# Where weight splits stand in the order of two engines at three changes of stage, in a two-block fp32 kernel

## The chip, the cores and the metric

The kernel runs on one core of one Trainium2 chip. The metric is the time of the program on the device in microseconds (us), as the median of several runs.

## The reference, cut to what matters

256 tokens of width 2048 pass through two blocks, each a mixer followed by a gated feed-forward part (FFN), in fp32. What matters here is what stands between the matrix products:

```
# block one                                   # block two
x1 = x + merged @ w_out                       h  = rms_norm(x2f, attn_norm_w, 1e-5)
h2 = rms_norm(x1, g_ffn)                      p  = h @ w_in_2
x2 = x1 + (silu(gate) * up) @ w_ffn_out       x3 = x2f + y @ w_out_2
x2f = rms_norm(x2, g_final, 1e-6)             h  = rms_norm(x3, ffn_norm_w) ; FFN as in block one
```

`rms_norm(x, g) = x * rsqrt(mean(x*x) + eps) * g`, over the 2048 columns of a token. Between the blocks two norms follow one another: x2 is normed with g_final, and the result, which is also block two's residual, is normed again with attn_norm_w.

## The kernel before, in words

**Products in three terms.** Each fp32 product `x @ w` is made of three matmul passes with a high and a low part of both sides: `xh*wh + xh*wl + xl*wh`. A weight matrix comes in chunks of 512 rows by 512 columns (1 MB, a tile of 128 x 2048). For every chunk SyncE issues a load into one of four ring slots (`raw[j % 4]`), ScalarE copies it to a high part (`hi[j % 2]`, two slots, L1339), VectorE subtracts to get the low part (`lo`, in place of the raw one, L1781), and TensorE runs 48 (`product`, L643 to L646) or 24 (`product_tokens`, L658 to L660) matmuls on it. A high part can be made only once the chunk two before is used up, a load can start once the chunk four before is.

**Order.** Every engine has its own program, written out by hand: nothing reorders it. An engine waits on semaphores in the order of that program, so a step that waits holds up all that stands behind it on the same engine. `Gemm` numbers chunks through the whole kernel; `chunks(g, i, j0, j1)` on ScalarE makes high parts, the function of the same name on VectorE low parts.

**A norm** before a product is split up by quarters (512 columns, 128 x 1024 elements). For each quarter: the residual is updated by VectorE from PSUM (L2057, L2125), ScalarE sums its squares (`squares`, L1323, two instructions and two reads of the sum), TensorE turns it (`turn_x`, L604, 8 transposes), VectorE multiplies by the gain column (`gained`, L1744, 4 instructions), ScalarE makes the high part of the activation (`high`, L1329), VectorE the low part (`low_part`, L1750). The root of the mean is applied behind the product: `inverse_root` makes it, `root_rows` writes it on a diagonal (L1771), TensorE spreads it over rows (`rstd_rows`, L630, behind the fourth chunk), and VectorE copies those rows out (L1774) for the strips to be scaled with.

**Changes of stage that matter here:**

- *Start.* `in1` (block one's input product) begins with four chunks, one for each quarter of the norm. Behind the fourth, TensorE turns parameters and spreads the root (L620, L630). VectorE's program then reads: root, `root_rows(0)` with its wait for TensorE, a copy of the parameters (L1847), and only then the low part of chunk 4.
- *Output product into FFN* (`wo1` into `up1`, `wo2` into `up2`), through `out_ffn`. The output product has four strips of four chunks. When a strip's end is two chunks back, ScalarE runs `residual_high`: `squares`, then `high`, which waits for `gained`, which waits for the turn, which TensorE does after the first chunk of the next strip. The high part of the weights that comes next stands behind that. The pattern occurs four times in each block.
- *FFN's down product into block two's input product* (`dn1` into `in2`). The last four chunks of `dn1` end one quarter each (`down_out`). A quarter of the residual gets x2 (`X`), then `XG = X * g_final` (L2127), which is what TensorE turns; the gain column is attn_norm_w. ScalarE sums the squares of both, `X` and `XG`. SyncE loads four chunks of `in2`, then waits for all sixteen sums of squares (`n_sq` at 16; the tiles share memory), loads two pieces of `w_lora` (L482, L483), and only behind them chunk 4 of `in2` and the rest. From the end of `dn1` on, GpSimd builds masks (L578, L540, L580).

`to_slot`, `f` and `taken` take strips out of PSUM. Waits such as `wait_ge(chunks_used, n)` mean that TensorE has finished chunk n.

Of the kernel before, what the change touches and what calls it, by code (L numbers as in the profile page):

```python
# [12 lines left out]
ALU = mybir.AluOpType  # L13
# [6 lines left out]
KT = D // P  # L20
# [48 lines left out]
def build(nc, a, out):  # L69
    ctx = ExitStack()  # L70
    with ctx:
# [527 lines left out]
        def _(pe):  # L599
# [160 lines left out]
            def downs(g, n, n_norm):  # L760
# [17 lines left out]

# [16 lines left out]
            def last_of_down():  # L795
                pe.wait_ge(xg_ready, 4)
                turn_x(3, 3, XG)

# [515 lines left out]
        def _(act):  # L1314
# [25 lines left out]

            def split(g, i, out_of, j0=0):

                for j in range(j0, g.per):
                    chunks(g, i, j, j + 1)
                    if j == 1 and not (isinstance(i, int) and i == 0):
                        out_of(i - 1, g.ns - 1)
                    elif j > 1 and j - 2 in g.ends:
                        out_of(i, g.ends[j - 2])

# [129 lines left out]

            def residual_high(g, n):  # L1480
                def f(i, s):
                    squares(2 * i + s, squared[1], strips_out, g.strip(i, s) + 1)
                    high(n, 2 * i + s, U[1])
                return f

            def ffn_sigmoid(g, n, i):
# [39 lines left out]
            out_ffn(wo1, up1, dn1, 1, 0, 2)  # L1526
            chunks(dn1, dn1.bodies - 1, 0, 4)

            for q in range(4):
                squares(q, squared[0], x_ready, 1 + q)  # L1530
                squares(q, squared2, xg_ready, 1 + q, XG, ssq2)
# [200 lines left out]
        def _(dve):  # L1732
# [34 lines left out]

            def root_rows(n):
# [3 lines left out]
                last.then_inc(n_diag, 1)  # L1772
                dve.wait_ge(n_sum, n + 1)
                V.tensor_copy(rstd[:], bank(7)[:, 0:T]).then_inc(rows_read, 1)  # L1774
# [96 lines left out]

            chunks(in1, 0, 4, 5)
            to_slot(0, 0)
# [246 lines left out]

            def down_out(g, q, count):

                dve.wait_ge(chunks_used, g.end - 3 + q)
                c = slice(q * CN, (q + 1) * CN)
                V.tensor_tensor(X[:, :, c], X[:, :, c], token_pair(q), ALU.add).then_inc(x_ready, 1)  # L2125
                dve.wait_ge(x_ready, count)
# [4 lines left out]
            chunks(dn1, dn1.bodies - 1, 0, 3)  # L2131
            dve.wait_ge(gain_landed, 16)
            down_out(dn1, 0, 1)
            chunks(dn1, dn1.bodies - 1, 3, 4)
            down_out(dn1, 1, 2)
            gained(2, 0, 0, U[0], "attn_norm_w_2")
            low_part(2, 0, U[0])
            down_out(dn1, 2, 3)
            gained(2, 1, 1, U[0], "attn_norm_w_2")
            low_part(2, 1, U[0])  # L2140
            chunks(in2, 0, 0, 1)
            down_out(dn1, 3, 4)
            gained(2, 2, 2, U[0], "attn_norm_w_2")
            low_part(2, 2, U[0])
            chunks(in2, 0, 1, 2)
            gained(2, 3, 3, U[0], "attn_norm_w_2")
            low_part(2, 3, U[0])
            chunks(in2, 0, 2, 4)
# [38 lines left out]

            chunks(in2, 0, 4, 5)
            f(0, 0)
            for t in range(2):  # L2190
# [408 lines left out]
```

## Time and profile before

| | us |
|---|---|
| median of 3 runs | 3015.83 (3013.49 to 3017.86) |
| the profiled execution: its own time | 3021.99 |
| its span in the trace | 3020.2 |
| TensorE busy (share of the span) | 2930.2 (97%), 18850 matmuls |
| VectorE busy | 1605.0 (53%) |
| ScalarE busy | 1165.7 (39%) |
| GpSimd busy | 49.5 (2%) |
| DMA, mean over the span | 166 GB/s |

The span is that of one execution; engine shares are averages over stages of different kinds. A matmul's duration in the trace reaches beyond the start of the next one, since they overlap: steps are best taken from start to start. The granted clock of TensorE is 1.00 where it runs at 2.4 GHz and 0.50 at 1.2 GHz.

### The profile page before, as it was taken

The numbers are of one execution on the slowest core, as the hardware profiler recorded it, in microseconds if no ns is written. First come the engines' busy times: TensorE is split into PE (matmuls) and PEld (weight loads), VectorE is DVE, ScalarE is ACT, GpSimd is POOL, SyncE is SP. The second block draws the span as 40 slices with busy tenths as digits, with TensorE's granted clock in tenths as the row PEclk, the third lists the DMA queues.
The fourth block names the chain that finished last, engine by engine and source line by source line (L and its number), as shares of the span: only waits on it lengthen the run. The fifth ranks groups of instructions, "written<-read, shape, count | busy, mean of one in ns | idle before, by whom it ended". The sixth has DMA issues, their size and how long they took to land.

```text
span 3020.2 us, 42955 instructions
## 1 busy us (share of the span) xinstructions
PE 2930.2 (97%) x18850; PEld 2521.2 (83%) x18850; DVE 1605.0 (53%) x1331; ACT 1165.7 (39%) x956; POOL 49.5 (2%) x119
## 2 busy tenths in 40 slices
PE   7999999999999999999999999899799999999998
PEld 7999788888778888888879999898677888888887
DVE  4657545445554545444455767754455454544445
ACT  3345443343443333433344433323234333343333
POOL 0000000000000000010001000000000000000000
PEclk9999999999999999999999999898799999999999
DMA  6556556666555555555554544100145555555554
GB/s 198 167 161 183 151 162 195 186 191 194 181 178 184 194 182 193 188 187 195 195 195 159 166 143 154 43 4 31 56 153 178 184 193 183 193 188 187 195 195 167
DMA packets 257288, 501.00 MB, mean 166 GB/s; under 512 B 12176, under 2 KB 17627, under 8 KB 256763
## 3 DMA queue, kind: packets, MB, share of 16 engines
q1 hardware_dynamic: 257147, 498.87, 51.4%
q8 instruction: 120, 1.97, 0.3%
q14 instruction: 21, 0.17, 0.0%
HBM read 496.74 MB, written 2.10 MB: 165 GB/s over the span
## 4 chain that ended last, share of the span: by engine, by line
PE 93%; DVE 5%; ACT 1%; issue 1%; DMA 0%; SPq 0%; ACTq 0%; DVEq 0%
PE psum L658 22%; PE psum L660 22%; PE psum L659 22%; PE psum L643 5%; PE psum L645 5%; PE psum L646 5%; PE psum L1070 3%; DVE weight_lo L1781 2%; ACT weight_hi L1339 1%; PE psum L956 1%; PE psum L709 1%; PE psum L950 0%; DVE u_ffn L1744 0%; PE psum L604 0%; DVE u_in L1744 0%
## 5 line engine op out<-in xcount | busy, mean ns | idle before, releaser
L1781 DVE TENSOR_TENSOR weight_lo<-weight_raw,weight_hi 128x2048 fp32r<-128x2048 f32 x460 | 1054.1, 2292 | 1141.4 <-ACT weight_hi L1339 1140.6
L1339 ACT ACTIVATE weight_hi<-weight_raw 128x2048 fp32r<-128x2048 f32 x460 | 881.0, 1916 | 1486.1 <-PE psum L660 1184.9
L658 PE MATMUL psum<-weight_hi,h_both 128*128 128x512 f32 x1856 | 725.3, 391 | 3.2 <-DVE weight_lo L1781 3.2
L660 PE MATMUL psum<-weight_hi,h_both 128*128 128x512 f32 x1856 | 722.5, 389 | 0.0
L659 PE MATMUL psum<-weight_lo,h_both 128*128 128x512 f32 x1856 | 722.1, 389 | 0.0
L643 PE MATMUL psum<-h_both,weight_hi 128*128 128x256 f32 x1408 | 406.9, 289 | 18.9 <-DVE weight_lo L1781 18.7
L658 PEld LDWEIGHTS psum<-weight_hi,h_both 128*128 128x128 f32 x1856 | 348.5, 188 | 75.1 <-issue 4.0
L660 PEld LDWEIGHTS psum<-weight_hi,h_both 128*128 128x128 f32 x1856 | 348.4, 188 | 72.7
L659 PEld LDWEIGHTS psum<-weight_lo,h_both 128*128 128x128 f32 x1856 | 348.6, 188 | 71.4
L645 PE MATMUL psum<-h_both,weight_lo 128*128 128x256 f32 x1408 | 403.2, 286 | 0.0
L646 PE MATMUL psum<-h_both,weight_hi 128*128 128x256 f32 x1408 | 403.0, 286 | 0.0
L643 PEld LDWEIGHTS psum<-h_both,weight_hi 128*128 128x128 f32 x1408 | 275.3, 196 | 25.0 <-issue 16.5
L645 PEld LDWEIGHTS psum<-h_both,weight_lo 128*128 128x128 f32 x1408 | 275.6, 196 | 0.1
L646 PEld LDWEIGHTS psum<-h_both,weight_hi 128*128 128x128 f32 x1408 | 275.1, 195 | 0.0
L658 PE MATMUL psum<-weight_hi,ffn_hi 128*128 128x512 f32 x672 | 261.9, 390 | 0.0
L660 PE MATMUL psum<-weight_hi,ffn_lo 128*128 128x512 f32 x672 | 261.4, 389 | 0.0
L659 PE MATMUL psum<-weight_lo,ffn_hi 128*128 128x512 f32 x672 | 261.4, 389 | 0.0
L660 PEld LDWEIGHTS psum<-weight_hi,ffn_lo 128*128 128x128 f32 x672 | 126.1, 188 | 26.4
L658 PEld LDWEIGHTS psum<-weight_hi,ffn_hi 128*128 128x128 f32 x672 | 126.1, 188 | 26.3 <-issue 0.6
L659 PEld LDWEIGHTS psum<-weight_lo,ffn_hi 128*128 128x128 f32 x672 | 126.1, 188 | 26.0
L660 PE MATMUL psum<-weight_hi,y_lo 128*128 128x512 f32 x320 | 126.3, 395 | 0.0
L658 PE MATMUL psum<-weight_hi,mixed_hi 128*128 128x512 f32 x256 | 103.4, 404 | 19.3 <-DVE weight_lo L1781 19.3
(512 smaller groups left out, 2305.6 us busy)
## 6 DMA issues: line engine op xcount, KB each, us to landing
weight_raw<-in_w_in SPq DMA_DIRECT2D x144, 1024.0 KB, 5.5
weight_raw<-in_w_ffn_in SPq DMA_DIRECT2D x88, 1024.0 KB, 5.0
weight_raw<-in_w_ffn_out SPq DMA_DIRECT2D x44, 1024.0 KB, 5.1
weight_raw<-in_ffn_w_gate SPq DMA_DIRECT2D x44, 1024.0 KB, 5.1
weight_raw<-in_ffn_w_up SPq DMA_DIRECT2D x44, 1024.0 KB, 5.1
weight_raw<-in_ffn_w_down SPq DMA_DIRECT2D x44, 1024.0 KB, 5.1
weight_raw<-in_w_out SPq DMA_DIRECT2D x32, 1024.0 KB, 5.1
weight_raw<-in_w_branch_rnn SPq DMA_DIRECT2D x8, 1024.0 KB, 5.1
```

What stands on the lines that cost most here:

```text
L643: mm(acc[:, f, :], wh[:, k, c], xh, start=(start and k == 0 and f % 2 == 0), stop=False, skip_group_check=True)
L645: mm(acc[:, f, :], wl[:, k, c], xh, start=False, stop=False, skip_group_check=True)
L646: last = mm(acc[:, f, :], wh[:, k, c], xl, start=False, stop=(stop and k == CK - 1), skip_group_check=True)
L658: mm(acc[:, t, :], xh[:, c], wh[:, k, :], start=(start and k == 0), stop=False, skip_group_check=True)
L659: mm(acc[:, t, :], xh[:, c], wl[:, k, :], start=False, stop=False, skip_group_check=True)
L660: last = mm(acc[:, t, :], xl[:, c], wh[:, k, :], start=False, stop=(stop and k == CK - 1), skip_group_check=True)
L709: last = tr(pair(2)[:, k, t * P:(t + 1) * P], act_up[:, t, k * P:(k + 1) * P], ident[:])
L956: last = mm(bank(b0 + (n - n0) // 2)[:, (n % 2) * T:(n % 2 + 1) * T], sel[:, n * P:(n + 1) * P], rows[:], start=(n % 2 == 0), stop=True, s ...
L1070: last = mm(o[r, u * 64:(u + 1) * 64], lhs(r, u0 + u), rhs(r, u0 + u), start=(u == 0), stop=True, skip_group_check=True)
L1339: A(hi[j % g.hi][:], raw[j % g.ring][:], ACT.Copy).then_inc(hi_ready, 1)
L1781: V.tensor_tensor(lo[r][:], raw[r][:], hi[j % g.hi][:].bitcast(F32), ALU.subtract).then_inc(lo_ready, 1)
```

## The change

Nothing is computed that was not before, but for one product of two columns of parameters; the number of matmuls, loads and table loads stays as it was. Cut to the core:

```diff
@@ TensorE: downs(), last_of_down() @@
-                            pe.wait_ge(xg_ready, j)
-                            turn_x(j - 1, j - 1, XG)
+                            pe.wait_ge(x_ready, j)
+                            turn_x(j - 1, j - 1, X)
...
@@ ScalarE: split() knows a later step, one chunk behind the first @@
+                    for d, f in ((2, out_of), (3, later)):
...
+                        if not first and j + g.per - d in g.ends:
+                            f(i - 1, g.ends[j + g.per - d])
+                        elif j >= d and j - d in g.ends:
+                            f(i, g.ends[j - d])
...
-                f = residual_high(wo, n_norm)
-                split(wo, 0, f, rhs)
-                split(wo, 1, f)
-                chunks(up, 0, 0, 2)
-                f(1, 1)
-                chunks(up, 0, 2, 4)
+                squared_of = lambda i, s: squares(2 * i + s, squared[1], strips_out, wo.strip(i, s) + 1)
+                high_of = lambda i, s: high(n_norm, 2 * i + s, U[1])
+                split(wo, 0, squared_of, rhs, high_of)
+                split(wo, 1, squared_of, 0, high_of)
+                chunks(up, 0, 0, 1)
+                chunks(up, 0, 1, 2)
+                squared_of(1, 1)
+                chunks(up, 0, 2, 3)
+                high_of(1, 1)
+                chunks(up, 0, 3, 4)
...
@@ ScalarE, dn1 into in2 @@
-            chunks(dn1, dn1.bodies - 1, 0, 4)
-            for q in range(4):
-                squares(q, squared[0], x_ready, 1 + q)
-                squares(q, squared2, xg_ready, 1 + q, XG, ssq2)
-                high(2, q, U[0])
-                if 0 < q < 3:
-                    chunks(in2, 0, q - 1, q)
-            chunks(in2, 0, 2, 4)
+            chunks(dn1, dn1.bodies - 1, 0, 3)
+            squares_x(0)
+            chunks(dn1, dn1.bodies - 1, 3, 4)
+            high(2, 0, U[0])
+            squares_x(1)
+            chunks(in2, 0, 0, 1)
+            squares_gained(0)
+            high(2, 1, U[0])
+            squares_x(2)
+            chunks(in2, 0, 1, 2)
+            high(2, 2, U[0])
+            squares_x(3)
+            chunks(in2, 0, 2, 3)
+            high(2, 3, U[0])
+            squares_gained(1)
+            chunks(in2, 0, 3, 4)
+            squares_gained(2)
+            squares_gained(3)
...
@@ VectorE: root_rows() is cut in two, the diagonals (root_diagonals) and the wait with the copy (root_rows) @@
             inverse_root(1, 4, EPS1)
+            root_diagonals()
+            chunks(in1, 0, 4, 5)
             root_rows(0)
...
-            chunks(in1, 0, 4, 5)
             to_slot(0, 0)
...
@@ VectorE, dn1 into in2: down_out() only updates X, times_gain() makes XG @@
+            settle(V.tensor_tensor(par1[:, c1:c1 + KT], par1[:, c1:c1 + KT], par1[:, c2:c2 + KT], ALU.mult))
...
+            chunks(dn1, dn1.bodies - 1, 0, 2)
+            down_out(0)
+            chunks(dn1, dn1.bodies - 1, 2, 3)
+            down_out(1)
+            next_gained(0)
+            chunks(dn1, dn1.bodies - 1, 3, 4)
...
+            times_gain(0)
+            down_out(2)
+            next_low(0)
+            next_gained(1)
+            chunks(in2, 0, 0, 1)
+            next_low(1)
+            down_out(3)
+            next_gained(2)
+            chunks(in2, 0, 1, 2)
+            next_low(2)
+            times_gain(1)
+            next_gained(3)
+            chunks(in2, 0, 2, 3)
+            next_low(3)
+            times_gain(2)
+            times_gain(3)
+            chunks(in2, 0, 3, 4)
...
-                root_rows(1)
+            root_diagonals()
...
             chunks(in2, 0, 4, 5)
+            root_rows(1)
             f(0, 0)
```

Here c1 and c2 are the columns of attn_norm_w and g_final: the gain that `next_gained` applies to the turned X is their product. What moves, in three places:

**ScalarE, output product into FFN, first strip.** raw2 is the slot of chunk 6, raw1 that of chunk 5, `squares_ffn` the squares of the first quarter, `h_both<-u_ffn` the high part of the activation. Before:

```order
L1339 ACTIVATE weight_hi1_58<-weight_raw1_50 128x2048
L1323 ACTIVATE squares_ffn_66,sum_squares_99<-residual_61 128x512 x2
L1329 ACTIVATE h_both_62<-u_ffn_64 128x1024
L1339 ACTIVATE weight_hi0_57<-weight_raw2_51 128x2048
L1339 ACTIVATE weight_hi1_58<-weight_raw3_52 128x2048
```

Changed:

```order
L1339 ACTIVATE weight_hi1_58<-weight_raw1_50 128x2048
L1323 ACTIVATE squares_ffn_66,sum_squares_99<-residual_61 128x512 x2
L1339 ACTIVATE weight_hi0_57<-weight_raw2_51 128x2048
L1329 ACTIVATE h_both_62<-u_ffn_64 128x1024
L1339 ACTIVATE weight_hi1_58<-weight_raw3_52 128x2048
```

The high part of chunk 6 has changed places with that of the activation; VectorE's order is the same in both there.

**VectorE, dn1 into in2.** raw2 and raw3 are the last two chunks of dn1, raw0 is the first of in2. Before:

```order
L1781 TENSOR_TENSOR weight_lo2_55<-weight_raw2_51,weight_hi0_57 128x2048
L2125 TENSOR_TENSOR residual_61<-residual_61,psum 128x2x512
L2127 TENSOR_TENSOR x_gained_68<-residual_61,gain_row_69 128x2x512
L1781 TENSOR_TENSOR weight_lo3_56<-weight_raw3_52,weight_hi1_58 128x2048
L2125 TENSOR_TENSOR residual_61<-residual_61,psum 128x2x512
L2127 TENSOR_TENSOR x_gained_68<-residual_61,gain_row_69 128x2x512
L1744 TENSOR_SCALAR u_in_63<-psum,par1_97 128x256 x4
L1750 TENSOR_TENSOR h_both_62<-u_in_63,h_both_62 128x1024
L2125 TENSOR_TENSOR residual_61<-residual_61,psum 128x2x512
L2127 TENSOR_TENSOR x_gained_68<-residual_61,gain_row_69 128x2x512
L1744 TENSOR_SCALAR u_in_63<-psum,par1_97 128x256 x4
L1750 TENSOR_TENSOR h_both_62<-u_in_63,h_both_62 128x1024
```

Changed:

```order
L2146 TENSOR_TENSOR residual_61<-residual_61,psum 128x2x512
L1801 TENSOR_TENSOR weight_lo2_55<-weight_raw2_51,weight_hi0_57 128x2048
L2146 TENSOR_TENSOR residual_61<-residual_61,psum 128x2x512
L1761 TENSOR_SCALAR u_in_63<-psum,par1_97 128x256 x4
L1801 TENSOR_TENSOR weight_lo3_56<-weight_raw3_52,weight_hi1_58 128x2048
L2152 TENSOR_TENSOR x_gained_68<-residual_61,gain_row_69 128x2x512
L2146 TENSOR_TENSOR residual_61<-residual_61,psum 128x2x512
L1767 TENSOR_TENSOR h_both_62<-u_in_63,h_both_62 128x1024
L1761 TENSOR_SCALAR u_in_63<-psum,par1_97 128x256 x4
L1801 TENSOR_TENSOR weight_lo0_53<-weight_raw0_49,weight_hi0_57 128x2048
L1767 TENSOR_TENSOR h_both_62<-u_in_63,h_both_62 128x1024
```

`x_gained` no longer stands in front of each turn, and the low part of in2's first chunk (raw0) has come ahead of the second `h_both`; before, it stands behind the last row shown.

**ScalarE, end of the same place.** Before, the last rows ahead of the root:

```order
L1329 ACTIVATE h_both_62<-u_in_63 128x1024
L1339 ACTIVATE weight_hi1_58<-weight_raw1_50 128x2048
L1323 ACTIVATE squares_in_65,sum_squares_99<-residual_61 128x512 x2
L1323 ACTIVATE squares_gained_67,sum_squares_gained_100<-x_gained_68 128x512 x2
L1329 ACTIVATE h_both_62<-u_in_63 128x1024
L1339 ACTIVATE weight_hi0_57<-weight_raw2_51 128x2048
L1339 ACTIVATE weight_hi1_58<-weight_raw3_52 128x2048
```

Changed:

```order
L1339 ACTIVATE weight_hi0_57<-weight_raw2_51 128x2048
L1329 ACTIVATE h_both_62<-u_in_63 128x1024
L1323 ACTIVATE squares_gained_67,sum_squares_gained_100<-x_gained_68 128x512 x2
L1339 ACTIVATE weight_hi1_58<-weight_raw3_52 128x2048
L1323 ACTIVATE squares_gained_67,sum_squares_gained_100<-x_gained_68 128x512 x4
```

The last sums of squares, which SyncE's wait counts, stand behind the high parts of all four first chunks of in2, where they stood behind those of the first two.

## Rows read from the trace of the kernel before

**Rows 1.** The page's waits of TensorE: engine, line, releaser: us in total, times, longest.

```profile
PE psum L658 <- DVE weight_lo L1781: 22.5, 10, 6.6
PE psum L643 <- DVE weight_lo L1781: 18.7, 10, 4.8
```

**Rows 2.** Timeline of TensorE, second strip of wo1: start, duration, instruction [idle before, releaser].

```profile
776.82 1.03 PE L604 MATMUL psum<-ident,residual 128*128 128x128 f32 x8
777.61 0.48 PE L658 MATMUL psum<-weight_hi,mixed_hi 128*128 128x512 f32 x1
...
784.83 0.50 PE L658 MATMUL psum<-weight_hi,mixed_hi 128*128 128x512 f32 x1 [1.52 <-DVE weight_lo L1781]
...
801.29 1.04 PE L604 MATMUL psum<-ident,residual 128*128 128x128 f32 x8
```

**Rows 3.** Timeline of ScalarE at the same place.

```profile
779.59 1.06 ACT L1329 ACTIVATE h_both<-u_ffn 128x1024 fp32r<-128x1024 f32 x1 [4.81 <-DVE u_ffn L1744]
780.55 1.90 ACT L1339 ACTIVATE weight_hi<-weight_raw 128x2048 fp32r<-128x2048 f32 x1
```

**Rows 4.** Timeline of VectorE at the same place.

```profile
777.89 1.66 DVE L1744 TENSOR_SCALAR u_ffn<-psum,par 128x256 f32<-128x256 f32 x4 [2.02 <-PE psum L604]
782.49 2.29 DVE L1781 TENSOR_TENSOR weight_lo<-weight_raw,weight_hi 128x2048 fp32r<-128x2048 f32 x1 [2.93 <-ACT weight_hi L1339]
```

**Rows 5.** Timeline of TensorE behind the fourth chunk of in1.

```profile
43.90 0.65 PE L630 MATMUL psum<-rstd_diag,ones 128*128 128x128 f32 x4
47.91 0.58 PE L643 MATMUL psum<-h_both,weight_hi 128*128 128x256 f32 x1 [3.36 <-DVE weight_lo L1781]
```

**Rows 6.** Timeline of VectorE and ScalarE at the same place.

```profile
44.58 0.42 DVE L1774 COPY rstd<-psum 128x256 f32<-128x256 f32 x1 [5.71 <-PE psum L630]
45.56 2.29 DVE L1781 TENSOR_TENSOR weight_lo<-weight_raw,weight_hi 128x2048 fp32r<-128x2048 f32 x1
...
38.06 1.90 ACT L1339 ACTIVATE weight_hi<-weight_raw 128x2048 fp32r<-128x2048 f32 x1
```

**Rows 7.** TensorE by stretches: start:end, length, busy (matmuls), granted clock, DMA share, GB/s.

```profile
47.91:62.26 14.35, 14.35 (x96) 0.79 0.82 246
1585.00:1593.00 8.00, 8.00 (x49) 0.69 0.00 1
1594.18:1600.01 5.83, 5.83 (x48) 1.00 0.85 285
1616.84:1624.84 8.00, 8.00 (x54) 0.79 0.14 52
2095.50:2109.00 13.50, 13.50 (x165) 0.51 0.00 1
...
2192.60:2200.60 8.00, 8.00 (x25) 0.69 0.01 2
```

**Rows 8.** Timeline of TensorE, dn1 into in2.

```profile
1566.37 1.09 PE L604 MATMUL psum<-ident,x_gained 128*128 128x128 f32 x8 [1.34 <-DVE x_gained L2127]
...
1585.00 0.55 PE L643 MATMUL psum<-h_both,weight_hi 128*128 128x256 f32 x1 [4.85 <-DVE weight_lo L1781]
...
1616.84 0.36 PE L643 MATMUL psum<-h_both,weight_hi 128*128 128x256 f32 x1 [2.94 <-DVE weight_lo L1781]
```

**Rows 9.** Waits of SyncE's queue, 1560 to 1660 us.

```profile
SPq L482 <- ACT squares_gained L1323: 14.5, 1, 14.5
```

**Rows 10.** Timeline of ScalarE, the last sum of squares and chunk 4 of in2.

```profile
1593.45 0.61 ACT L1323 ACTIVATE squares_gained<-x_gained 128x512 f32<-128x512 f32 x1
...
1607.89 1.91 ACT L1339 ACTIVATE weight_hi<-weight_raw 128x2048 fp32r<-128x2048 f32 x1 [1.64 <-DMA weight_raw<-in_w_in]
```

**Rows 11.** Timeline of VectorE and of GpSimd while the masks are built.

```profile
1586.02 1.23 DVE L2127 TENSOR_TENSOR x_gained<-residual,gain_row 128x1024 f32<-128x1024 f32 x1
1591.74 2.29 DVE L1781 TENSOR_TENSOR weight_lo<-weight_raw,weight_hi 128x2048 fp32r<-128x2048 f32 x1 [0.58 <-ACT weight_hi L1339]
...
1580.11 16.48 POOL L540 TENSOR_SCALAR_AFFINE_SELECT chunk_masks_upper<-chunk_masks_upper 128x64 f32<-128x64 f32 x28
```

More of the change, by code:

```diff
@@ L795, in last_of_down @@
             def last_of_down():
-                pe.wait_ge(xg_ready, 4)
-                turn_x(3, 3, XG)
+                pe.wait_ge(x_ready, 4)
+                turn_x(3, 3, X)
             def forget_logits():
@@ L1339, in chunks, with split @@
                     A(hi[j % g.hi][:], raw[j % g.ring][:], ACT.Copy).then_inc(hi_ready, 1)
-            def split(g, i, out_of, j0=0):
+            def split(g, i, out_of, j0=0, later=None):
                 for j in range(j0, g.per):
                     chunks(g, i, j, j + 1)
[L1345 to L1348, printed above, removed]
+                    first = isinstance(i, int) and i == 0
+                    for d, f in ((2, out_of), (3, later)):
+                        if f is None:
+                            continue
+                        if not first and j + g.per - d in g.ends:
+                            f(i - 1, g.ends[j + g.per - d])
+                        elif j >= d and j - d in g.ends:
+                            f(i, g.ends[j - d])
             def strip_done(e, g, i, s):
@@ L1478, in _ @@
             merged_high(3)
[L1480 to L1484, printed above, removed]
             def ffn_sigmoid(g, n, i):
@@ L1526, in _, with squares_x, squares_gained @@
             out_ffn(wo1, up1, dn1, 1, 0, 2)
-            chunks(dn1, dn1.bodies - 1, 0, 4)
-            for q in range(4):
+            def squares_x(q):
                 squares(q, squared[0], x_ready, 1 + q)
+            def squares_gained(q):
                 squares(q, squared2, xg_ready, 1 + q, XG, ssq2)
-                high(2, q, U[0])
-                if 0 < q < 3:
-                    chunks(in2, 0, q - 1, q)
-            chunks(in2, 0, 2, 4)
+            chunks(dn1, dn1.bodies - 1, 0, 3)
[16 more added lines that the diff above has]
+            squares_gained(3)
             root(3, rcol1)
@@ L1766, in inverse_root, with root_diagonals @@
                 dve.wait_ge(ready, made)
-            def root_rows(n):
+            def root_diagonals():
                 for t in range(2):
@@ L1772, in root_rows @@
                 last.then_inc(n_diag, 1)
+            def root_rows(n):
                 dve.wait_ge(n_sum, n + 1)
@@ L2119, in out_ffn, with down_out, times_gain @@
                     chunks(dn, i, 0, 4)
-            def down_out(g, q, count):
-                dve.wait_ge(chunks_used, g.end - 3 + q)
+            def down_out(q):
+                dve.wait_ge(chunks_used, dn1.end - 3 + q)
                 c = slice(q * CN, (q + 1) * CN)
                 V.tensor_tensor(X[:, :, c], X[:, :, c], token_pair(q), ALU.add).then_inc(x_ready, 1)
-                dve.wait_ge(x_ready, count)
+            def times_gain(q):
+                c = slice(q * CN, (q + 1) * CN)
+                dve.wait_ge(x_ready, q + 1)
                 V.tensor_tensor(XG[:, :, c], X[:, :, c], gain_row[:, c].unsqueeze(1).to_broadcast([P, 2, CN]),
@@ L2130, in _ @@
             out_ffn(wo1, up1, dn1, 1, "g_ffn", EPS1, 0, 3)
-            chunks(dn1, dn1.bodies - 1, 0, 3)
-            dve.wait_ge(gain_landed, 16)
[L2133 to L2140, printed above, removed]
+            c1, c2 = col["attn_norm_w_2"], col["g_final"]
+            settle(V.tensor_tensor(par1[:, c1:c1 + KT], par1[:, c1:c1 + KT], par1[:, c2:c2 + KT], ALU.mult))
+            next_gained = lambda q: gained(2, q, q, U[0], "attn_norm_w_2")
+            next_low = lambda q: low_part(2, q, U[0])
+            chunks(dn1, dn1.bodies - 1, 0, 2)
[4 more added lines that the diff above has]
+            chunks(dn1, dn1.bodies - 1, 3, 4)
+            dve.wait_ge(gain_landed, 16)
+            times_gain(0)
+            down_out(2)
+            next_low(0)
+            next_gained(1)
             chunks(in2, 0, 0, 1)
-            down_out(dn1, 3, 4)
-            gained(2, 2, 2, U[0], "attn_norm_w_2")
-            low_part(2, 2, U[0])
+            next_low(1)
+            down_out(3)
+            next_gained(2)
             chunks(in2, 0, 1, 2)
-            gained(2, 3, 3, U[0], "attn_norm_w_2")
-            low_part(2, 3, U[0])
-            chunks(in2, 0, 2, 4)
+            next_low(2)
[6 more added lines that the diff above has]
+            chunks(in2, 0, 3, 4)
             inverse_root(3, 16, EPS1, rcol1)
```

## The prediction, made before the changed kernel ran

> **What bounds the kernel now.** I read the page first: TensorE is busy 97% of the span, so time can only come from its pauses, from what they do to its clock, or from its work, which stays as it is. The waits of TensorE then say who ends the pauses: twenty waits on `weight_lo`, 41.2 us together [rows 1]. The timelines say where they are. Four of 1.5 to 1.6 us stand in each passage from the output product to the FFN (one of them: [rows 2]), one of 3.36 us behind the start's fourth chunk [rows 5], and pauses of 1.34, 4.85 and 2.94 us in the passage from dn1 to in2 [rows 8]. These are the places that the change touches. The rest of the 41.2 us (6.62 us before wo2 above all) it leaves alone.
>
> The windows show the second price of a pause [rows 7]. At granted clock 1.00, which is 2.4 GHz, 48 matmuls take 5.83 us, 0.1215 us each. Behind the 4.85 us pause 49 of them take 8.00 us instead of 5.95, since the clock stands at 1.2 GHz for some of it: 2.05 lost. By the same sum 2.7 us are lost behind the 3.36 us pause (96 in 14.35 instead of 11.66) and 1.4 behind that of 2.94 (54 in 8.00 instead of 6.56). Behind the 6.62 us before wo2 it is 2.3 (25 of the 512-wide, at 0.228 each [rows 2]: 5.7 instead of 8.00).
>
> **Part A, output product into FFN, eight places.** In one of them the turn begins at 776.82, the next chunk at 777.61, the chunk after that at 784.83, and the next turn at 801.29 [rows 2]. The last three chunks so take 16.46, 5.49 each; the first would take about as much, 5.54 with the slower first matmuls behind a turn, and end at 783.15. The place costs 784.83 - 783.15 = 1.68, and some 0.1 for the restart. Cause: ScalarE holds `high` for 4.81 us until `gained` is done at 779.55, and only then makes the high part of chunk 6, at 780.55 [rows 3, 4]; VectorE has the low part from 782.49 to 784.78 [rows 4]. In the changed order nothing holds that high part back but its slot, free when the turn begins at about 776.9: done 778.8. VectorE still has `gained` in front (to 779.55), so the low part is done at 779.55 + 2.25 = 781.8, 1.35 us ahead of need. `high` follows at 779.6 to 780.65, `low_part` behind the weight's low part to 783, the next chunk's high part at 783.3, when its slot comes free, as before. Nothing new is late. Bounds for a place: 1.5 (the pause alone) and 1.8; I take 1.75, since the starts bear it out. **Eight places: 14.0 us** (12.2 to 14.4).
>
> **Part B, start.** The high part of chunk 4 is done at 39.96, the rows are copied only at 44.58 behind 5.71 us of waiting, and the low part begins at 45.56 [rows 6]. Now it stands ahead of the wait: 40.0 to 42.3. TensorE goes on when its last transposes let it, 0.15 us before their recorded end at 44.55, so at 44.4 instead of 47.91 [rows 5]: 3.5 us. The clock's 2.7 go too. VectorE's copies and the first strip's evacuation then end near 46.8, the low part of chunk 5 near 49.4, and TensorE needs it at 44.4 + 5.8 = 50.2. **6.2 us** (3.5 if the clock falls all the same).
>
> **Part C, dn1 into in2.** Here the early steps gain much and the end gives most of it back. TensorE no longer waits for `x_gained`: the turn follows at 1564.9 instead of 1566.37, its last turn in dn1 comes at 1577.6, and in2 could start at 1578.4, if chunk 0's low part is there. VectorE, in the new order with durations start to start of 1.2 (residual and gain) [rows 11], 1.6 (`gained`) and 2.2 (low part of weights) [rows 4], and 1.15 (low part of the activation, a tile of the size of x_gained): from 1571.4, when the second turn has freed the third quarter, its steps follow with no gap. The third residual, low 0, gained 1 and chunk 0's low part end at 1577.6. So in2 starts at 1578.4 instead of 1585.00, 6.6 us earlier and at 2.4 GHz. Its four chunks end at 1584.2, 1590.9, 1596.7 and 1602.5 (5.83 each, [rows 7], one turn between the first two); the low parts of chunks 1, 2 and 3 are done at 1583.8, 1590.0 and 1595.8, each ahead of need, by 0.9 to 1.2 us.
>
> But then chunk 4 is missing. SyncE's queue waited 14.5 us for the last sum of squares [rows 9], and the loads of w_lora and of chunk 4 stand behind that wait. The last sum ends at 1594.06, ScalarE finds chunk 4 at 1607.89 [rows 10], 13.83 us later, with TensorE's speed having no part in it. In the new order the last sum comes *later*: from 1571.4 VectorE has 5 x 1.2 + 4 x 1.15 + 3 x 1.6 + 3 x 2.2 = 22.0 us to do up to the last x_gained, 1593.4; ScalarE makes chunk 3's high part to 1592.9 (its slot is freed at 1590.9) and the last two pairs of squares to 1595.3. Then 13.8 for the loads, 1.9 for the high part [rows 10], 2.3 for the low part [rows 4] and 0.2 of handshakes: TensorE starts chunk 4 at 1613.6 instead of 1616.84. It has stood since 1603.1, 10.5 us, longer than any pause shown, and the clock will fall. Earlier start 3.2; the loss at 1616.84, 1.4, goes; one of about 2.3, as behind the 6.62 us pause, comes. **2.3 us.** Bounds: if each of the four activation low parts waits 1.1 us for ScalarE, as it does between `gained` and `low_part` before, the last sum comes 4.4 later and the part gives -2.1; if the clock stays up, +4.6. The product of the two gain columns (0.2 us) and the later rows of the root lie beside the wait for chunk 4 and cost nothing; should that cover go, they have the 10.5 us pause to fill first.
>
> Masks are built during this. x_gained (1.23) and a weight's low part (2.29) run at their usual speed while GpSimd works from 1580.11 to 1596.6 [rows 11], so I take VectorE's durations as they are. The Trainium skill speaks against that: the GPSIMD Engine Reference, Specifications, says that GpSimd shares its SBUF interfaces with VectorE and contends with VectorE's instructions that have two SBUF inputs. By that rule x_gained and both kinds of low part would slow down under the masks; it is a rival below.
>
> **Sum.** 14.0 + 6.2 + 2.3 = 22.5 us. The profiled execution took 3021.99 (span 3020.2 and 1.8 around it), so it would take 2999.5; it lies 6.2 above the median of 3015.83, so **the median goes to 2993.3**.
>
> **Rivals.**
> 1. *The last sum is later than I make it* (ScalarE and VectorE wait for one another in the dense new order, up to the bound above). Part C gives about -1: 2996.6. For it: `low_part` waited for `high` at every quarter before. Against: weight parts now fill those waits. 0.10.
> 2. *VectorE still comes late in part A*, since `gained` stays in front of chunk 6's low part and the margin is 1.35 us. Half of A remains: 3000.3. Against: all eight places have the same rows within 0.05 us. 0.08.
> 3. *Chunk 4 does not bind*: then the 10.5 us pause and the 2.3 lost behind it go too, and C is worth 15.1: 2980.5. Against: the queue's wait and the 13.83 us behind it [rows 9, 10], whose order the change leaves. 0.03.
> 4. *GpSimd slows VectorE.* From 1579 to 1594 three gain steps of 1.2, two low parts of weights of 2.2 and three of activations of 1.15 would double, 11.4 us, and the last sum is that much later: C gives 3.2 - 11.4 + 1.4 - 2.3 = -9.1, so 3004.7. Against: the speeds under the masks [rows 11]. 0.02.
> 5. *Slower:* the clock stays down after the pause before chunk 4. To end over 6 us slower it must lose 28.5 us more than I reckon, which at 1.2 GHz takes 57 us of running; with 60, 3023. For it: the pause is longer than any I have rows for. Against: the longest low stretch found is 13.5 us [rows 7], and behind 6.62 us the clock was back within 8. 0.04. The skill's page TensorE: Matmul & The Clock Gate, Seeing it yourself, warns that the gate has been seen stuck at a low setting for over 50 us; with 50, an estimate by that page, C would lose 25 and the time come to about 3016, no change.
> 6. *No effect within 6 us*: the pauses move to other chunks. 0.03.
>
> **How the numbers follow.** My forecast gets 0.70. About 0.2% (6 us) is what a measurement of this kernel can tell from no change. Faster by more: the forecast and rivals 1 to 4, 0.70 + 0.10 + 0.08 + 0.03 + 0.02 = 0.93; same 0.03; slower 0.04. The range goes from 2986 (the forecast with A and C at their upper ends, 2.7, less 2 for the chain of part C and 2 for the medians' own spread) to 3003 (rivals 1 and 2, plus 2 to 3 of spread); rivals 3 to 6 lie outside, 0.12.
>
> **What would show it.** Right: no wait of 1.5 us on `weight_lo` between turns of `residual` in either passage, and turns there 22.7 apart instead of 24.5; no pause at 44 us; in2's first chunk starting near 1565 (1578.4 less block one's half of A, 7.0, and B, 6.2) at clock 1.00, chunks 0 to 3 in one run; then one pause of about 10 us, ended by a low part whose high part waited for a load; SyncE still waiting for `squares_gained`. Wrong: a pause before chunk 4 shorter than 6 us or longer than 14, waits on `weight_lo` left in part A, or low clock for more than 10 us behind the pause.

## The result, and the profile after

Over four runs of each in turn, the changed kernel took 2993.29 us (median; 2987.71 to 2997.93) and the kernel before 3016.69 (3013.49 to 3017.86). The ratio is 0.9924, 95% interval 0.9906 to 0.9942: faster by 23.4 us, where 22.5 was forecast. The profiled execution took 2997.93 with a span of 2996.2, which is 24.0 less than the span before.

The page's first part, its waits of TensorE (rows of part 5) and SyncE's queue between 1545 and 1645 us (engine, line, releaser: us in total, times, longest), answer to [rows 1, 9]:

```profile
PE 2923.0 (98%) x18850; PEld 2518.7 (84%) x18850; DVE 1604.5 (54%) x1332; ACT 1166.9 (39%) x956; POOL 53.0 (2%) x119
...
L643 PE MATMUL psum<-h_both,weight_hi 128*128 128x256 f32 x1408 | 404.8, 288 | 16.3 <-DVE weight_lo L1801 16.3
...
L658 PE MATMUL psum<-weight_hi,mixed_hi 128*128 128x512 f32 x256 | 102.4, 400 | 10.2 <-DVE weight_lo L1801 10.2
```

```profile
SPq L482 <- ACT squares_gained L1323: 17.3, 1, 17.3
```

The work of every engine is the same. TensorE's waits on low parts of weights fell from 41.2 us to 26.5. Of these 9.9 are one new pause and 6.6 the one before wo2, which the change leaves alone. SyncE now waits longer for the sums of squares than before (17.3 for 14.5).

**Output product into FFN.** TensorE around the same turn as in [rows 2]; the four chunks between the second row and the next turn have no pause among them:

```profile
770.75 1.03 PE L604 MATMUL psum<-ident,residual 128*128 128x128 f32 x8
771.54 0.48 PE L658 MATMUL psum<-weight_hi,mixed_hi 128*128 128x512 f32 x1
...
793.41 0.82 PE L604 MATMUL psum<-ident,residual 128*128 128x128 f32 x6
```

ScalarE and VectorE there, the rows that answer to [rows 3, 4]:

```profile
771.01 1.92 ACT L1339 ACTIVATE weight_hi<-weight_raw 128x2048 fp32r<-128x2048 f32 x1 [2.31 <-PE psum L660]
773.52 1.07 ACT L1329 ACTIVATE h_both<-u_ffn 128x1024 fp32r<-128x1024 f32 x1 [0.59 <-DVE u_ffn L1761]
```

```profile
771.83 1.66 DVE L1761 TENSOR_SCALAR u_ffn<-psum,par 128x256 f32<-128x256 f32 x4 [2.02 <-PE psum L604]
773.40 2.28 DVE L1801 TENSOR_TENSOR weight_lo<-weight_raw,weight_hi 128x2048 fp32r<-128x2048 f32 x1
```

The high part of the weights begins 0.26 us after the turn, when its slot comes free, not 3.7 after it. The low part ends at 775.68. The chunk that wants it follows the one begun at 771.54, which takes 5.54, so from 777.08: 1.4 us to spare. From turn to turn it is 22.66 instead of 24.47.

**Start.** VectorE makes the low part at 40.18 and only then waits for the rows, and TensorE's next chunk stands directly behind its transposes:

```profile
40.18 2.29 DVE L1801 TENSOR_TENSOR weight_lo<-weight_raw,weight_hi 128x2048 fp32r<-128x2048 f32 x1 [1.12 <-ACT weight_hi L1339]
44.76 0.42 DVE L1794 COPY rstd<-psum 128x256 f32<-128x256 f32 x1 [2.29 <-PE psum L630]
```

```profile
44.08 0.65 PE L630 MATMUL psum<-rstd_diag,ones 128*128 128x128 f32 x4
44.48 0.36 PE L643 MATMUL psum<-h_both,weight_hi 128*128 128x256 f32 x1
```

**dn1 into in2.** TensorE, where [rows 8] had three pauses:

```profile
1564.25 1.04 PE L604 MATMUL psum<-ident,residual 128*128 128x128 f32 x8
1565.05 0.36 PE L643 MATMUL psum<-h_both,weight_hi 128*128 128x256 f32 x1
...
1599.54 0.55 PE L643 MATMUL psum<-h_both,weight_hi 128*128 128x256 f32 x1 [9.91 <-DVE weight_lo L1801]
```

The first chunk of in2 starts 19.95 us earlier than before (1585.00); 13.3 of them were won ahead of this place, by A and B. Four chunks run without a break. Then one pause of 9.91 us comes, and behind it the clock is low for a while. The windows (columns as in [rows 7], with the busy time of every engine after the length: TensorE, its weight loads, VectorE, ScalarE, GpSimd) show equal lengths after the start's fourth chunk, at full clock, and behind this pause:

```profile
44.48:56.16 11.68, 11.68 (x99) 11.55 (x97) 8.46 (x16) 4.90 (x4) 0.00 (x0) 1.00 0.98 289
1599.54:1611.22 11.68, 11.68 (x80) 11.68 (x81) 7.61 (x6) 5.03 (x5) 0.00 (x0) 0.80 0.50 167
```

80 matmuls at 0.1215 us are 9.7, so 2.0 of the 11.68 were lost. ScalarE says why the pause is there, as in [rows 10]: the last sum of squares, the read of it, and chunk 4 of in2, which it finds 13.1 us behind the end of the squares at 1582.03 (13.83 before):

```profile
1581.42 0.61 ACT L1323 ACTIVATE squares_gained<-x_gained 128x512 f32<-128x512 f32 x1
...
1595.16 1.91 ACT L1339 ACTIVATE weight_hi<-weight_raw 128x2048 fp32r<-128x2048 f32 x1 [10.23 <-DMA weight_raw<-in_w_in]
```

SyncE's own rows show what lies between the two:

```profile
1582.15 0.37 SPq L482 DMA_DIRECT2D w_lora<-in_w_in  x1
1582.56 2.03 SPq L483 DMA_DIRECT2D w_lora<-in_w_in  x1
1584.64 40.60 SPq L460 DMA_DIRECT2D weight_raw<-in_w_in  x8
```

The first of the eight loads in the last row is chunk 4's. It lands 10.5 us after its issue, where the median of such loads is 5.5. Just ahead of it stand 2.4 MB of w_lora, which land 8.8 and 9.2 us after theirs; that they are what makes it late is read from these times, not tested. Before, the same load took 11.4.

**Where the 24.0 us of the two spans went**, by starts on TensorE:

| stretch | before | after | less |
|---|---|---|---|
| start to the forget logits (L802) | 62.26 | 56.16 | 6.10 |
| L802 to wo1's first turn | 714.56 | 714.59 | -0.03 |
| wo1's first to fourth turn | 73.41 | 68.00 | 5.41 |
| fourth turn to the first w_lora product (L914) | 802.72 | 797.45 | 5.27 |
| L914 to wo2's first chunk | 539.65 | 539.39 | 0.26 |
| from there to wo2's first turn | 18.74 | 18.96 | -0.22 |
| wo2's first to fourth turn | 73.49 | 67.99 | 5.50 |
| fourth turn to the end | 735.37 | 733.66 | 1.71 |

Each place of part A is worth 1.80 (5.41 / 3), and the fourth place of each block lies in the row below its three. So A has 5.41 + 1.80 + 5.50 + 1.71 = 14.4, B 6.1, and C 5.27 - 1.80 = 3.5.

### The profile page after: what moved, and what is told of

It reads as the page before. It is cut to its first block, busy times and chain, and to the rows that moved or that the text cites. A ratio compares the mean times of both kernels' runs of the same rounds, so it can differ in the third digit from the quotient of the medians.

```text
span 2996.2 us, 42957 instructions
## 1 busy us (share of the span) xinstructions
PE 2923.0 (98%) x18850; PEld 2518.7 (84%) x18850; DVE 1604.5 (54%) x1332; ACT 1166.9 (39%) x956; POOL 53.0 (2%) x119
## 4 chain that ended last, share of the span: by engine, by line
PE 95%; DVE 3%; ACT 1%; DMA 0%; issue 0%; SPq 0%; DVEq 0%; ACTq 0%
PE psum L658 23%; PE psum L660 23%; PE psum L659 23%; PE psum L643 5%; PE psum L645 5%; PE psum L646 5%; PE psum L1070 3%; PE psum L956 1%; DVE weight_lo L1801 1%; PE psum L709 1%; PE psum L950 0%; PE psum L604 0%; DMA weight_raw<-in_w_in 0%; ACT weight_hi L1339 0%; PE psum L1034 0%; PE psum L872 0%
## 5 line engine op out<-in xcount | busy, mean ns | idle before, releaser
L658 PEld LDWEIGHTS psum<-weight_hi,ffn_hi 128*128 128x128 f32 x672 | 126.1, 188 | 26.5 <-issue 0.6
```

The source lines that it names most:

```text
L658: mm(acc[:, t, :], xh[:, c], wh[:, k, :], start=(start and k == 0), stop=False, skip_group_check=True)
```

## Experiments

Every kernel here computes all of the reference. "C's stretch" is the time from wo1's fourth turn to L914, with 1.8 us added for kernels that have part A, so that it compares with the 802.7 of before. The kernel before was run beside every batch: 3019.69 for the first four labels, 3015.90 for the next four, 3018.05 for the last two.

**The parts one by one.** Each is the kernel before with one part of the change put in, and `changed_again` is the changed kernel. `...` in a diff stands for lines that are not shown.

`only_strips` (part A):

```diff
...
-                split(wo, 1, f)
-                chunks(up, 0, 0, 2)
-                f(1, 1)
-                chunks(up, 0, 2, 4)
+                split(wo, 1, squared_of, 0, high_of)
+                chunks(up, 0, 0, 1)
+                chunks(up, 0, 1, 2)
+                squared_of(1, 1)
+                chunks(up, 0, 2, 3)
+                high_of(1, 1)
+                chunks(up, 0, 3, 4)
```

`only_start` (part B):

```diff
             inverse_root(1, 4, EPS1)
+            root_diagonals()
+            chunks(in1, 0, 4, 5)
             root_rows(0)
...
-            chunks(in1, 0, 4, 5)
             to_slot(0, 0)
```

`only_between` (part C) has the turns of X, both new orders from dn1 to in2, and the later rows:

```diff
-                            turn_x(j - 1, j - 1, XG)
+                            turn_x(j - 1, j - 1, X)
...
-            root_rows(1)
+            root_diagonals()
...
             chunks(in2, 0, 4, 5)
+            root_rows(1)
```

> The kernel before with part A alone (ScalarE makes the high part of chunk 6 ahead of that of the activation). My theory: the eight pauses of 1.5 us on weight_lo go, turn to turn falls from 24.5 to 22.7 us, the time falls by 14.0 to 14.4 us; the start and the passage from dn1 to in2 keep their pauses (3.36, 4.85, 2.94 us). Rival (VectorE comes late all the same): half of it, 7 us. Rival (the strips only pay together with the rest): under 3 us.

> The kernel before with part B alone (low part of chunk 4 of in1 ahead of the wait for the spread root). My theory: the pause of 3.36 us at 44 us goes and with it the low clock behind it, so 6.1 us: 3.4 for the pause and 2.7 for the clock. Rival (the clock falls there all the same, from what ran before): 3.4 us only.

> The changed kernel with parts A and B undone: part C alone. My theory: in2's first chunk starts 6.6 us earlier against the turns of dn1 and chunk 4 only 3.2 to 4.0 us earlier, behind a pause of about 10 us ended by the load; net 3.0 to 3.7 us, within the noise of the medians. Rival (the gain of 6.6 us and the clock carry through): 10 us or more.

> The changed kernel once more, on the chip of the other three. If the parts are independent, its gain over the kernel before is the sum of the three: 14.2 + 6.1 + 3.7 = 24 us by the trace, 0.8%. The four runs seen spread over 10 us (2987.7 to 2997.9), those before over 4.4. If that spread is the pause's, it shows in the length of the pause before chunk 4 or in the clock behind it.

| | median (runs) | range | ratio to before [95%] | span of the profile |
|---|---|---|---|---|
| only_strips | 3002.74 (6) | 2993.46 to 3012.46 | 0.9941 [0.9917, 0.9965] | 3010.5 |
| only_start | 3010.60 (10) | 3001.16 to 3016.02 | 0.9975 [0.9964, 0.9987] | 2999.4 |
| only_between | 3013.84 (10) | 3004.40 to 3022.99 | 0.9984 [0.9971, 0.9998] | 3005.2 |
| changed_again | 2993.55 (4) | 2988.19 to 2997.45 | 0.9920 [0.9903, 0.9936] | 2986.5 |

The three ratios multiplied give 0.9900, with some 0.003 of uncertainty, against 0.9920: the parts add up within what the runs can tell, and each is a gain by itself, `only_between` just clear of none. The traces are sharper than the medians. `only_strips` has its turns 22.67 us apart and no other pause gone (it reaches L802 at 61.45, for 62.26 before; C's stretch is 803.9). `only_start` reaches L802 at 55.77. In `only_between` C's stretch is 800.1, 2.6 less than before where 3.0 to 3.7 was expected, with this row in place of the pause of 2.94:

```profile
1612.38 0.55 PE L643 MATMUL psum<-h_both,weight_hi 128*128 128x256 f32 x1 [10.20 <-DVE weight_lo L1799]
```

How far C's stretch can be trusted shows in four kernels in which nothing in it should change, and which all keep the pause of 2.94 us: 802.7 before and in `only_start`, 803.9 in `only_strips`, 801.3 in `loads_ahead_before` below. Behind that pause the same 288 matmuls up to L914 take 36.11, 36.08, 37.27 and 34.63 us, at granted clocks of 0.95, 0.95, 0.92 and 1.00. So differences of the stretch under some 1.3 us say nothing.

The single spans are a warning: `only_start` has a profile 20.8 us shorter than before's, though its own place gives 6.5. The last section says where that comes from.

**Is the 9.91 us pause the load of chunk 4?** By my account SyncE's wait for the sums holds it back. So let two more chunks be loaded ahead of that wait, in the changed kernel (`loads_ahead`) and in the kernel before (`loads_ahead_before`):

```diff
-            load(in2, 0, 0, 4)
+            load(in2, 0, 0, 6)
             sp.wait_ge(n_sq, 16)
...
-            load(in2, 0, 4)
+            load(in2, 0, 6)
```

> The changed kernel, with SyncE issuing the loads of chunks 4 and 5 of in2 ahead of its wait for the sixteen sums of squares (before, behind the wait and behind w_lora). My theory: that wait is what holds chunk 4 back, so the 9.9 us pause goes and the low clock behind it (2.1 us): 12 us faster than the changed kernel, about 2981 by medians; w_lora lands at its old time and is not needed earlier, chunk 6 lands just in time. Rival (something else holds chunk 4, VectorE's rows of the root or ScalarE's order): a pause of over 5 us stays. Rival (w_lora or chunk 6 come late instead): the pause moves to chunk 6, and 3 to 8 us are gained.

> The same edit of SyncE's order on the kernel before. My theory: there the pause of 2.94 us before chunk 4 is ended by VectorE, whose low part stands behind its wait for the spread root (high part ready since 1609.8, low part begun at 1614.4), so the earlier load changes nothing: 0 +- 1 us. Rival (the load binds there too): 3 to 4 us faster.

`loads_ahead` took 2983.19 (2975.98 to 2985.85, four runs), ratio 0.9888 [0.9870, 0.9906]: the lowest median of all kernels here, about 10 us below the changed one. SyncE's wait fell to 4.1 us, since the queue reaches it later, and TensorE goes from the fourth chunk's transposes straight into chunk 4; one pause of 0.60 us stands before chunk 5.

```profile
SPq L482 <- ACT squares_gained L1323: 4.1, 1, 4.1
```

```profile
1588.43 0.61 PE L630 MATMUL psum<-rstd_diag,ones 128*128 128x128 f32 x4
1588.81 0.36 PE L643 MATMUL psum<-h_both,weight_hi 128*128 128x256 f32 x1
1595.40 0.39 PE L643 MATMUL psum<-h_both,weight_hi 128*128 128x256 f32 x1 [0.60 <-DVE weight_lo L1801]
```

C's stretch is 788.0, 11.3 below the changed kernel's. So the pause is the load's. The edit takes chunk 4 past two things at once, though, SyncE's wait and w_lora. No kernel here leaves it behind the wait and ahead of w_lora. By an estimate from the rows above it would then be issued at 1582.15 and land 5.5 us later, 7.5 us sooner than it did, and most of the pause would go; w_lora is first used at 1603.47. The same edit in the kernel before did nothing: 3018.86 (3013.41 to 3022.17, ten runs), ratio 1.0005 [0.9994, 1.0016], C's stretch 801.3, which is the clock's doing as said above. ScalarE now made chunk 4's high part when TensorE freed its slot (this row of its timeline), 5.50 us ahead of the transposes at 1609.94. In [rows 10], where it waited for the load, it was 5.40 ahead of them, so the load had been 0.1 late. TensorE's pause stayed to the hundredth:

```profile
1604.44 1.92 ACT L1339 ACTIVATE weight_hi<-weight_raw 128x2048 fp32r<-128x2048 f32 x1 [1.56 <-PE psum L646]
```

```profile
1613.48 0.36 PE L643 MATMUL psum<-h_both,weight_hi 128*128 128x256 f32 x1 [2.94 <-DVE weight_lo L1781]
```

So the 2.94 us in the kernel before were not the load's. VectorE in `loads_ahead_before` shows whose they were: its copy of the rows waits 6.79 us for TensorE's transposes, and the low part of chunk 4 stands behind it.

```profile
1610.59 0.42 DVE L1774 COPY rstd<-psum 128x256 f32<-128x256 f32 x1 [6.79 <-PE psum L630]
1611.05 2.29 DVE L1781 TENSOR_TENSOR weight_lo<-weight_raw,weight_hi 128x2048 fp32r<-128x2048 f32 x1
```

**Are the rows of the root the cause?** `only_rows_later` moves nothing else in the kernel before; `rows_early_again` puts them back in the changed one.

```diff
             settle(V.tensor_tensor(rcol[:], rcol[:], rcol1[:], ALU.mult))
-            root_rows(1)
+            root_diagonals()
...
             chunks(in2, 0, 4, 5)
+            root_rows(1)
             f(0, 0)
```

> The kernel before, with root_rows(1) moved behind the low part of chunk 4 of in2 and nothing else. My theory: the 2.94 us pause shrinks to 0 to 0.3 us (high part 1609.8, low part to 1612.1, TensorE there at 1613.2) and the 1.4 us lost to the clock go: 4.3 us faster, as much as all of part C nets. Rival: the load or ScalarE hold chunk 4 to about the same time, under 1 us.

> The changed kernel, with root_rows(1) back ahead of the low part of chunk 4 of in2. My theory: TensorE spreads the root at 1589.0 and the high part of chunk 4 is ready only at 1597.1, so the copy is long done: same as the changed kernel within 0.3 us in the trace. Rival: the order of the two costs something here too, 1 to 4 us slower.

In `only_rows_later` the pause is gone:

```profile
1613.20 0.61 PE L630 MATMUL psum<-rstd_diag,ones 128*128 128x128 f32 x4
1613.57 0.36 PE L643 MATMUL psum<-h_both,weight_hi 128*128 128x256 f32 x1
```

C's stretch is 799.0, 3.7 less than before: this one line gives as much as the whole of part C (3.5; 2.6 in `only_between`), as far as the stretch can tell. The median is 3016.61 (3010.65 to 3018.00, ten runs), ratio 0.9992 [0.9982, 1.0002], too little to tell by runs alone. In `rows_early_again` the stretch is 798.6 with a pause of 9.99, and the median 2991.21 (2982.04 to 2997.97, four runs), ratio 0.9916 [0.9884, 0.9947]: in the changed kernel, where the load is last, the place of the rows is worth nothing.

**Both small edits without part C.** If they did it all, part C's new order would be idle. `loads_and_rows_before` is the kernel before with both:

```diff
-            load(in2, 0, 0, 4)
+            load(in2, 0, 0, 6)
...
             chunks(in2, 0, 4, 5)
+            root_rows(1)
```

> The kernel before with both small edits: loads of chunks 4 and 5 of in2 ahead of SyncE's wait, and root_rows(1) behind the low part of chunk 4. It closes the square of four: reorder of part C or not, loads ahead or not. My theory: without the reorder TensorE does not get to chunk 4 before 1613.2, so the loads ahead add nothing to the 3.7 us that the rows give: last turn of wo1's stage to the first product with w_lora 799.0 us, as without them. With the reorder they took it from 797.5 to 786.2. Rival (loads ahead are worth 11 us by themselves): 788.

The stretch is 799.0 again, the median 3015.34 (3008.21 to 3018.01, ten runs), ratio 0.9986 [0.9976, 0.9996]. With rows and loads out of the way the new order is worth 799.0 - 788.0 = 11.0 us, and all of it comes from its early steps. Counted from wo1's fourth turn, in2's first chunk starts 6.7 us earlier (728.1 us behind it with the 1.8 added, for 734.8), where [rows 8] had pauses of 1.34 and 4.85, and from there to the root's transposes TensorE needs 23.97 instead of 28.29 us. Without the loads ahead all of that is given back in one pause.

**Or bring the last sum forward.** In the changed kernel `sums_early` makes all of x_gained and its squares before the last quarter of the activation, and leaves the loads where they are.

```diff
             chunks(in2, 0, 2, 3)
-            high(2, 3, U[0])
             squares_gained(1)
-            chunks(in2, 0, 3, 4)
             squares_gained(2)
             squares_gained(3)
+            high(2, 3, U[0])
+            chunks(in2, 0, 3, 4)
...
             times_gain(1)
+            times_gain(2)
+            times_gain(3)
             next_gained(3)
```

> The changed kernel with SyncE's order as it is, but the last three x_gained and their sums of squares ahead of the last activation quarter on VectorE and ScalarE. My theory (the wait for the sixteen sums holds chunk 4 back): the last sum comes about 5.3 us earlier (1576.7 for 1582.0 in the changed kernel's trace), a pause of about 1.4 us appears before chunk 2 of in2, and chunk 4 starts 5 us earlier all the same, with a pause of 3 to 5 us before it instead of 10. Rival (chunk 4 comes when its load has time in the queues, whatever the sums): chunk 4 starts at the same time or, with the new pause, 1.4 us later.

Median 2989.99 (2983.84 to 2993.59, four runs), ratio 0.9891 [0.9875, 0.9908]. TensorE's timeline has two pauses:

```profile
1578.64 0.36 PE L643 MATMUL psum<-h_both,weight_hi 128*128 128x256 f32 x1 [1.24 <-DVE weight_lo L1801]
...
1595.24 0.55 PE L643 MATMUL psum<-h_both,weight_hi 128*128 128x256 f32 x1 [4.40 <-DVE weight_lo L1801]
```

SyncE's wait fell from 17.3 to 11.9, the last sum was 5.4 us earlier, chunk 2 came 1.24 late as expected, and chunk 4 started 4.1 earlier than in `changed_again`, both counted from wo1's fourth turn. Of the 5.4 us 1.3 were lost on the way, since chunk 4 was found 14.5 us behind the last squares, not 13.2: its load landed 11.9 us after its issue, not 10.5. C's stretch is 795.2, 4.2 less than 799.4 in `changed_again` and 7.2 more than in `loads_ahead`, which the ratios (0.9891 and 0.9888) do not tell apart. The chain of last sum, queue and load is shown from both of its ends: the pause shrinks with an earlier sum, and goes with an earlier load.

## Why the prediction held, and where it did not

**The total, 22.5 forecast, 23.4 by medians and 24.0 by spans.** That the medians came within 1 us is partly luck: the interval of the ratio reaches from 17.5 to 28.4 us. The parts, read from stretches of the trace, are what the forecast can be held against.

**Part A, 14.0 forecast, 14.4 measured (14.5 in `only_strips`' turns).** The mechanism held at all eight places. The low part's margin was 1.4 us where 1.35 was reckoned. The term was 1.75 a place and each gave 1.80, the upper bound: 0.28 went beside the pause of 1.52, where the 1.75 leaves 0.23.

**Part B, 6.2 forecast, 6.1 measured.** TensorE went on at 44.48 (44.4 forecast), and the low clock is gone. But the second half of that term was partly luck. Six kernels with the old start show how long TensorE needs from its restart to L802: 14.35, 14.33, 13.10, 13.07, 12.99 and 11.70 us, against 11.68 without a pause. Behind the same pause of 3.36 us the clock costs from nothing to 2.7, 1.6 on average. I took one execution's 2.7 for the price. By that average B is worth about 3.6 + 1.6 = 5.2, with 3.6 for the restart, which comes 6.50 us behind the start of the fourth chunk (37.98) instead of 10.12 (37.79).

**Part C, 2.3 forecast, 3.5 measured.** Step by step, with the forecast's times moved by its own 13.2 us of A and B:

| | forecast | measured |
|---|---|---|
| first chunk of in2 | 1565.2 | 1565.05 |
| last squares end | 1582.1 | 1582.03 |
| from there to chunk 4 found | 13.8 | 13.1 |
| chunk 4 starts | 1600.4 | 1599.54 |
| pause before it | 10.5 | 9.91 |
| clock lost behind it | 2.3 | 2.0 |

The step that was mis-sized is the passage of the load, 13.8 for 13.1, and the clock took 0.3 less; that is nearly all of the 1.2. The passage is no constant: the landing of chunk 4's load, behind w_lora, is 10.5 us of it here, and it was 11.4 before and 11.9 in `sums_early`. Nor is 3.5 sharper than the 1.3 us by which C's stretch varies: `changed_again` gives 3.3, `only_between` 2.6.

One step failed in substance, though it cost the sum nothing. I wrote of the later rows of the root that they "lie beside the wait for chunk 4 and cost nothing", and for the kernel before I named only the load as what chunk 4 waits for, which makes the pause of 2.94 us the load's. It belonged to those rows. Before, chunk 4's high part was done at 1609.8 [rows 10], so its low part could have ended at 1612.1, and TensorE came for it only behind the root's transposes of 1613.29. Before, too, VectorE stood waiting for those transposes, with the low part behind the wait:

```profile
1613.29 0.61 PE L630 MATMUL psum<-rstd_diag,ones 128*128 128x128 f32 x4
```

```profile
1613.94 0.42 DVE L1774 COPY rstd<-psum 128x256 f32<-128x256 f32 x1 [6.79 <-PE psum L630]
1614.40 2.29 DVE L1781 TENSOR_TENSOR weight_lo<-weight_raw,weight_hi 128x2048 fp32r<-128x2048 f32 x1
```

The end of the pause was right for the changed kernel alone, because there the load is later than either. So the forecast held the total, and would have been wrong about any smaller version of the change: the rows alone give 3.7, the loads alone nothing.

**Rivals.** *The last sum later* did not come: the squares ended within 0.1 us of the forecast, and the four activation low parts never waited for ScalarE. *VectorE late in A*: no pause at any place. *Chunk 4 does not bind*: it does, but the price set for it was right. I gave C 15.1 us without that pause, and `loads_ahead` has 802.7 - 788.0 = 14.7. *The clock stays down*: 2.0 us were lost. *No effect*: no. *GpSimd slows VectorE*: not here. The masks now run from 1565.25, under nearly all of VectorE's chain, and its steps take what they took:

```profile
1565.25 19.85 POOL L540 TENSOR_SCALAR_AFFINE_SELECT chunk_masks_upper<-chunk_masks_upper 128x64 f32<-128x64 f32 x28
```

```profile
1571.38 1.25 DVE L2152 TENSOR_TENSOR x_gained<-residual,gain_row 128x1024 f32<-128x1024 f32 x1
...
1574.12 2.32 DVE L1801 TENSOR_TENSOR weight_lo<-weight_raw,weight_hi 128x2048 fp32r<-128x2048 f32 x1
...
1585.36 1.68 DVE L1788 TENSOR_SCALAR rstd_diag<-ident,rstd_col 128x128 f32<-128x128 f32 x2
```

1.25 and 2.32 us stand against 1.23 and 2.29 [rows 11]. The Trainium skill's GPSIMD Engine Reference, Specifications, has the two engines contend over their SBUF interfaces for just such instructions; for these masks the trace shows 1 to 2% of it on VectorE's side.

## What to carry to other kernels

When work is moved earlier in front of a wait that stays, the gain is paid back at that wait: look up what is queued behind it, and whether it needs the wait at all, and move that too (here two loads on SyncE's queue, 10 us in the medians, for a change of two numbers). A pause names only its last link, so before a pause is put down to one cause, look at what the engine that ends it was itself waiting for, and check that the suspected input was in fact late. And small edits of a few us are better judged by one stretch of the trace, from one landmark to the next, than by medians of a kernel whose executions differ by 10 us in another place, once kernels that leave the stretch alone have shown how much it varies by itself.

## What the runs showed of the hardware that I had not expected

**The same work takes two lengths.** From L914 to wo2's first chunk all twelve profiles run the same instructions. Seven took 537.6 to 544.1 us, five 525.0 to 529.4, with no relation to the part of the change that they have. The windows show a difference of granted clock, in `only_strips` and in `changed_again`:

```profile
1646.07:2190.18 544.11, 503.81 (x6864) 467.09 (x6863) 337.42 (x444) 181.34 (x215) 7.71 (x8) 0.91 0.26 83
```

```profile
1636.61:2165.87 529.26, 488.94 (x6865) 456.81 (x6863) 337.42 (x444) 181.41 (x215) 7.73 (x8) 0.94 0.27 85
```

And it falls where TensorE has no pause, in the middle of a row of narrow products (`g_up`, each second one with 32 rows). In `only_strips`:

```profile
1729.43 0.70 PE L943 MATMUL psum<-lora,g_up 128*128 128x256 f32 x2
1730.06 0.69 PE L944 MATMUL psum<-lora,g_up 32*128 32x256 f32 x2
1730.68 1.06 PE L943 MATMUL psum<-lora,g_up 128*128 128x256 f32 x2
1731.67 1.22 PE L944 MATMUL psum<-lora,g_up 32*128 32x256 f32 x2
```

The granted clock is 1.00 from 1720 to 1726 and 0.50 from 1731 to 1739. In `changed_again` the same products, as far behind L914, ran at 0.69 and 0.70 a pair to the end. The windows of 16 us there, again `only_strips` first, have granted clocks of 0.57 and 1.00, so that 0.43 x 16 = 6.9 us were lost:

```profile
1730.00:1746.00 16.00, 16.00 (x54) 10.41 (x54) 4.69 (x2) 2.06 (x4) 0.00 (x0) 0.57 0.02 8
```

```profile
1720.60:1736.60 16.00, 16.00 (x105) 13.01 (x105) 6.86 (x3) 3.99 (x5) 0.00 (x0) 1.00 0.22 72
```

This stretch is most of how the span of `only_start` came to lie 20.8 us below that of before: 14.6 of it between L914 and wo2, 6.5 in its own place. It is of the size of the spread among runs of one kernel (7 to 19 us), which leaves intervals of 3 to 9 us either way. What decides in which executions the clock falls here stays open; no run was made for it.

**GpSimd is slowed, VectorE hardly.** The same 28 masks took 16.48 us before [rows 11], and 16.47 or 16.48 in all six kernels without part C's order; they took 19.85 after, and 19.84 to 20.15 in all six with it, in which VectorE works beside them without gaps. That VectorE is the cause was not tested by itself. VectorE's two-operand steps kept their speed within 2%. The one that did not is the small `rstd_diag`, 1.68 us for two instead of 0.48, and it began 0.17 us behind GpSimd's joining of the masks (L580, from 1585.19, 1.58 us). In the four other kernels in which it began 0.18 or 0.19 behind it, it took 1.68 to 1.71; in `sums_early` it was done 0.6 us ahead of it and took 0.48. It cost nothing here, since TensorE wanted its result only at 1589.
